# Two chained blocks on one core: silu of block two's convolution channels on ScalarE, a third value buffer, and later slots on TensorE for the sums of squares

## The reference, cut to what matters

```
u = rms_norm(h, norm_mix)
proj = u @ w_in                                   # 1024 x (512 + 4*512 + 8)
pool_out = pool_mixer(proj[..., :P], w_pool, pool_scale)
qkv = causal_conv_silu(proj[..., P:P + 3*G], conv_w)      # 4 taps over time, then silu
z = proj[..., P + 3*G:P + 4*G];  a, b = the last 8 columns
q, k are then l2-normalised per head of 128 channels: t * rsqrt(sum(t*t) + EPS)
```

## Time and profile before

| | |
|---|---|
| three runs, us | 2588.22, 2595.64, 2595.78; median 2595.64 |
| profiled execution | 2589.21 us, of it 2587.5 us span |
| busy shares | PE 93%, PEld 74%, DVE 71%, ACT 42%, POOL 28% |
| mean granted TensorE clock | 0.971 of full speed |
| first tap of channel 5 to first tap of channel 13 | 1452.22 to 1571.34 us of the span |

### The profile page before, as it was taken

The page is one execution under the profiler, slowest core; times in us unless marked ns, Lnnn a source line. Parts: engine busy times, 40 slices in busy tenths (PEclk is TensorE's granted clock), DMA queues, the critical chain, the costliest instruction groups (busy, mean ns, idle before and its releaser), DMA issues.

```text
span 2587.5 us, 35017 instructions
## 1 busy us (share of the span) xinstructions
PE 2396.1 (93%) x13848; PEld 1905.2 (74%) x13848; DVE 1829.8 (71%) x2431; ACT 1075.7 (42%) x1616; POOL 721.2 (28%) x737
## 2 busy tenths in 40 slices
PE   3988969879999999999999999888999999999998
PEld 3966823457778788888887767677787878888887
DVE  6358988885577798778865685466447678877775
ACT  5135468854343344433343442233234334444333
POOL 1432277505455211111032223323453310000000
PEclk8999979989999999999999999999999999999999
DMA  6200155224223545454433111001231353555542
GB/s 234 74 17 17 42 147 127 83 66 141 70 67 122 189 137 191 175 187 150 133 99 112 36 38 33 2 2 35 66 122 57 114 203 131 187 179 179 174 145 80
DMA packets 173850, 282.20 MB, mean 109 GB/s; under 512 B 13407, under 2 KB 86900, under 8 KB 173686
## 3 DMA queue, kind: packets, MB, share of 16 engines
q1 hardware_dynamic: 160336, 259.57, 30.9%
q10 hardware_dynamic: 13350, 20.38, 2.2%
HBM read 252.52 MB, written 27.33 MB: 108 GB/s over the span
## 4 chain that ended last, share of the span: by engine, by line
PE 72%; DVE 14%; issue 5%; ACT 5%; POOL 4%; DMA 1%; SPq 0%; ACTq 0%; DVEq 0%; POOLq 0%
PE ps L2927 20%; PE ps L2916 16%; PE ps L2621 5%; PE ps L2622 5%; PE ps L2623 5%; PE ps L2606 4%; PE ps L2608 3%; PE ps L2607 3%; PE ps L3096 2%; DVE yt L2429 2%; PE ps L2697 1%; DVE w_lo L2132 1%; DVE yt L2418 1%; DVE raw L2149 1%; PE ps L2777 1%
## 5 line engine op out<-in xcount | busy, mean ns | idle before, releaser
L1471 ACT ACTIVATE w_hi<-raw 128x1024 fp32r<-128x1024 f32 x198 | 209.0, 1057 | 366.9 <-DVE raw L2149 163.4
L2132 DVE TENSOR_TENSOR w_lo<-raw,w_hi 128x1024 fp32r<-128x1024 f32 x198 | 259.5, 1311 | 126.2 <-ACT w_hi L1471 125.9
L2927 PE MATMUL ps<-w_hi,us_hi 128*128 128x512 f32 x784 | 308.8, 394 | 15.4 <-DVE u_f L2158 9.9
L2927 PE MATMUL ps<-w_lo,us_hi 128*128 128x512 f32 x784 | 308.0, 393 | 0.0
L2927 PE MATMUL ps<-w_hi,us_lo 128*128 128x512 f32 x784 | 307.4, 392 | 0.0
L2606 PE MATMUL ps<-h_hi,w_hi 128*128 128x512 f32 x704 | 286.7, 407 | 8.8 <-issue 4.3
L2608 PE MATMUL ps<-h_hi,w_lo 128*128 128x512 f32 x704 | 276.4, 393 | 0.0
L2607 PE MATMUL ps<-h_lo,w_hi 128*128 128x512 f32 x704 | 276.3, 393 | 0.0
L2182 DVE TENSOR_TENSOR x<-x,ps 128x512 f32<-128x512 f32 x392 | 247.4, 677 | 0.1
L1033 POOL TENSOR_TENSOR raw<-raw,gate 128x1024 f32<-128x1024 f32 x32 | 93.6, 2946 | 378.0 <-DMA raw<-in_w_down_dram 378.0
L2927 PEld LDWEIGHTS ps<-w_hi,us_hi 128*128 128x128 f32 x784 | 147.7, 188 | 53.2 <-DVE u_f L2158 11.6
(11 more groups left out here) (488 smaller groups left out, 5318.3 us busy)
## 6 DMA issues: line engine op xcount, KB each, us to landing
h_all<-h_t SPq DMA_DIRECT2D x96, 512.0 KB, 5.5
h_extra<-h_t SPq DMA_DIRECT2D x96, 512.0 KB, 6.7
raw<-in_w_up_dram SPq DMA_DIRECT2D x64, 512.0 KB, 3.9
raw<-in_w_down_dram SPq DMA_DIRECT2D x64, 512.0 KB, 6.2
raw<-in_w_ada_dram SPq DMA_DIRECT2D x48, 512.0 KB, 4.2
raw<-in_w_in_dram SPq DMA_DIRECT2D x32, 512.0 KB, 3.8
raw<-in_w_out_dram SPq DMA_DIRECT2D x32, 512.0 KB, 3.9
h_t<-ht_hi ACTq DMA_DIRECT2D x32, 256.0 KB, 2.3
```

The costliest lines, as they stand in the source:

```text
L1471: s.activation(w_hi[:, slot, :], raw[:, r, :], ACT.Copy).then_inc(sem("w_hi_done"), 1)
L2132: v.tensor_tensor(w_lo[:, slot, :], raw[:, r, :], w_hi[:, slot, :].bitcast(F32), ALU.subtract).then_inc(sem("split_done"), 1)
L2927: last = mm(ps[:, b, :], l[:, c, tok], r, start=(fresh and c == 0 and n == 0), stop=(c == 1 and n == 2), skip_group_check=True)
```

## The change: what it does

ScalarE evaluates silu itself (`ACT.Silu`) where it evaluated the sigmoid, so VectorE's product at L2433 is dropped and `conv_silu` is counted by ScalarE. The value buffer of channel i becomes one of three; the third is `zc[:, 0, :]`, which is free until channel 16 but for the pool groups' intermediate values. The first tap of channel i waits for channel i - 3 instead of i - 2. On TensorE the product into banks 6 and 7 of channel j stands before `cm` of channel j + 2 for pool groups 0 to 2 (the same place in the stream as before), and inside `cm` of channel j + 2 for the others: after 4 of its 16 steps for pool group 3, after 2 of them for q and k.

```
-                y = yt[:, i % 2, :]
+                y = y_of[i]
...
+        AUX_STEP = {i: 0 for i in range(GH - 1)}
+        AUX_STEP[GH - 1] = 4
+        AUX_STEP.update({GH + j: 2 for j in range(2 * GH)})
+        y_of = [(yt[:, 0, :], yt[:, 1, :], zc[:, 0, :])[i % 3] for i in range(len(CH2))]
...  (ScalarE)
-                    if i >= 2 and ch_free[i - 2]:
-                        act.wait_ge(sem(ch_free[i - 2][0]), ch_free[i - 2][1])
+                    if i >= 3 and ch_free[i - 3]:
+                        act.wait_ge(sem(ch_free[i - 3][0]), ch_free[i - 3][1])
...
                     act.wait_ge(sem("taps"), 3 * (c + 1))
-                    s.activation(chunk_of(c), y, ACT.Sigmoid).then_inc(sem("conv_sig"), 1)
+                    s.activation(chunk_of(c), y, ACT.Silu).then_inc(sem("conv_silu"), 1)
...  (VectorE)
-                if i < len(CH2) and kind == "qkv":
-                    dve.wait_ge(sem("conv_sig"), c + 1)
-                    v.tensor_tensor(chunk_of(c), chunk_of(c), y, ALU.mult).then_inc(sem("conv_silu"), 1)
...  (TensorE)
+            def aux(i):
+
+                kind, c = CH2[i]
+                if i == 0:
+                    pe.wait_ge(sem("ab_out"), 2)
+                elif (i - 1) in aux_read:
+                    pe.wait_ge(sem(aux_read[i - 1][0]), aux_read[i - 1][1])
+                y = y_of[i]
+                if kind == "pool":
+                    pe.wait_ge(sem("gs_in"), 48)
+                    pe.wait_ge(sem("pooled"), 2 * (c + 1))
+                else:
+                    pe.wait_ge(sem("l2_sq"), c + 1)
+                for half in range(2):
+                    last = mm(ps[:, 6 + half, :], wpool[:, c, :] if kind == "pool" else ones,
+                              y[:, half * HALF:(half + 1) * HALF], start=True, stop=True)
+                last.then_inc(sem("pool_mm" if kind == "pool" else "l2_mm"), 1)
+
+            def aux_in(i, half):
+
+                def after(k):
+                    if AUX_STEP.get(i - 2) == NK * half + k + 1:
+                        aux(i - 2)
+                return after
+
+            for i in range(len(CH2)):
+                if AUX_STEP.get(i - 2) == 0:
+                    aux(i - 2)
...
-                        cm(i, half, 2 * (i % 3) + half, None, "cm2_full", 2 if i == 0 else None)
+                        cm(i, half, 2 * (i % 3) + half, aux_in(i, half), "cm2_full", 2 if i == 0 else None)
```

More of the change, by code:

```diff
@@ L1630, in aux_out, with first_tap @@
                                  bias=eps2 if c < GH else eps).then_inc(sem("l2_sd"), 1)
+            def first_tap(i):
+                c = CH2[i][1]
+                s.activation(y_of[i], pair(i), ACT.Copy,
+                             scale=cw2[:, 3 * 12 + c:3 * 12 + c + 1]).then_inc(sem("tap0"), 1)
             for i in range(len(CH2) + 1):
@@ L1643, in _ @@
                     if kind == "qkv":
-                        s.activation(y, pair(i), ACT.Copy,
-                                     scale=cw2[:, 3 * 12 + c:3 * 12 + c + 1]).then_inc(sem("tap0"), 1)
+                        first_tap(i)
                     if kind == "z":
@@ L2426, in _ @@
                     if kind1 == "qkv" and c1 < 2 * GH:
-                        y1 = yt[:, (i - 1) % 2, :]
+                        y1 = y_of[i - 1]
                         dve.wait_ge(sem("l2_sd"), c1 + 1)
@@ L3032, in _ @@
             pe.wait_ge(sem("norm_lo"), 5 * NK + 6)
-            for i in range(len(CH2) + 1):
+            def aux(i):
[4 more added lines that the diff above has]
+                    pe.wait_ge(sem(aux_read[i - 1][0]), aux_read[i - 1][1])
+                y = y_of[i]
+                if kind == "pool":
[15 more added lines that the diff above has]
+                    aux(i - 2)
                 if i < len(CH2):
@@ L3055, in _ @@
                     mm(ps[:, 6, 32:64], blk, g32, start=True, stop=True).then_inc(sem("gs_mm"), 1)
[L3056 to L3071, removed]
             pe.wait_ge(sem("z_silu"), GH - 1)
```

## The result

The changed kernel takes 2573.89 us in the median of six runs, the kernel before 2588.8 us in the median of six; the medians lie 14.9 us apart. The ratio, which is that of the means of these runs, is 0.9934, with a 95% interval of 0.9917 to 0.9951. That is 17 us less (13 to 21 by the interval). The profiled execution took 2572.14 us, with a span of 2570.4 us.

What follows compares the result with a forecast made beforehand. PE was taken to bound most of the kernel, a loop through ACT and DVE the eight q and k rounds; 8 x 12.65 = 101.2 instead of 119.12 us gains 17.9, so 2595.64 - 17.9 = 2577.7, forecast 2577, range 2569 to 2584.

Steps and rivals of the forecast that it cites:

- The hole and its loop: Eight q and k rounds: a loop through ACT and DVE makes periods of 14.89 us, PE waiting 11.4 us for squares.
- Sum: Eight q and k rounds at PE's pace, 101.2 instead of 119.12 us; the whole 17.9 us reach the end.
- Silu: ACT in each round: silu taken at 1.06 us like the sigmoid; only over 5.8 us would it lengthen the period.
- Table loads: ACT: if silu is in another set, beta's sigmoid and first z add one load each in idle time, cost 0.
- The order within a round: Times after T, the end of `cm` of a channel on PE; DVE has 1.0 us of slack each round.
- The later slot and the third buffer: Sums of squares inside channel i + 1 on PE, price 1.75 us as before; third buffer cost 0.
- Masks: GpSimd, behind v's last silu: masks take 13.4 us, and 11.6 us of slack before first use stays.
- Rival A: q and k rounds: hand-overs eat the slack, the loop becomes DVE's, 13.5 us gained, 2582; chance 0.08.
- Rivals B to E: B: product dearer inside channels, 2590, 0.06; C: lost later, 2581, 0.04; D: clock falls, 2679, 0.02; E: unchanged, 2595, 0.03.

Runs made afterwards that it cites:

- the one-pass sums: Changed kernel with q and k squares rounded to fp32r and summed by two one-pass matmuls instead of four float32 passes: 2561.93 us, ratio 0.9895; with old slot 2560.08.
- the same cut by order alone: Kernel before with only VectorE's silu product moved ahead of the reciprocal, two buffers, old slot: 2587.85 us, one run.

## Why the prediction was right

The forecast was 2577 us, 0.993 of the kernel before, and the measured ratio is 0.9934. By its own steps:

- *The hole and its loop.* Right. Rounds of 14.89 us became 12.65, and the run with DVE's load restored outside the loop lost nothing.
- *Sum.* 17.9 us were worked out, 17.94 lie between the first taps. Outside them the profiled execution is 1.42 us longer ahead and 0.6 us shorter behind, within the scatter of the executions. The absolute time lies 3 us lower than forecast. The median of before, 2595.64 then, is 2588.8 with three more runs, and 2588.8 - 17.9 would be 2570.9; the median of the changed kernel lies 3 us over that. How near 2577 came to it is thus in part a matter of the scatter. The sum against the profiled execution gave 2571.3, and 2572.14 was measured.
- *Silu.* 1.06 us, as the nearest row. The Trainium skill, "ScalarE: Activation LUTs", "Step-by-step: what each stage is for", says that the function doesn't change the throughput, and the trace agrees.
- *Table loads.* Silu and sigmoid are in different sets: beta's sigmoid got a load at 1450.04 and the first z one at 1582.77. Both lie in idle time, as forecast. The load again starts 0.02 us after the instruction before it, and the next, where it need not wait for another engine, 0.01 to 0.02 behind it; the drain that the Trainium skill adds in "ScalarE: Activation LUTs", "What ACT_TABLE_LOAD costs", is not seen.
- *The order within a round.* The product on PE was put at T+1.4, the square root at T+3.3 and the end of the square at T+7.9, with 1.0 us of slack on DVE. With T = 1466.04, a quarter before the first tap, the rows have T+1.4, T+3.3 and T+7.9, and 1.01 us.
- *The later slot and the third buffer* were each costed at 0 for the path. Right, but the slot's reason was not needed: at its old place the sum costs nothing either in the kernel with silu alone, and 0.37 us with the one-pass sums.
- *Masks.* They start at 1582.81 and end at 1596.16, used at 1609.02: 12.9 us of slack, 11.6 forecast; the silu of v comes a little earlier because the product on DVE is gone.

Where it was wrong is in the rivals. Rival A and the slack it rests on charged any round of DVE over 12.65 us at once to the end: "8 x 1.7 = 13.5 us gained". Silu alone ran 12.88 us rounds, and the run with one more product 12.8 to 15.1 on DVE, at no cost. The slack of 1.0 us is only that of the first tap; PE needs the square 5 to 6 us after it is ready, and a lag has to use that up before PE waits. I had the 6 us in the text ("6 us earlier") and did not use it in the rival. Rivals B to E are not seen: the product takes 1.88 us within a channel as between two, the stretch from z to the end is no longer, the clock rose to 1.00, and no wait of PE took the place of the old one.

## What to carry to other kernels

When two engines take turns in hand-ordered streams, look for the loop through both: here one short product behind a long reciprocal held the next round's first instruction, and 18 us came from cutting that, not from the work saved. Then look for the loop that is next in length: with two buffers the same cut by order alone gave 2.3 us. Count slack to the engine that sets the end, and over all rounds: a round that is 0.2 us too long for eight rounds costs nothing when 5 us are in hand. The other parts of an edit may then be idle, as the third buffer was, until the bound moves: with PE's round 1.3 us shorter it carried 7 us.

## What was not expected of the hardware

DVE and GpSimd held each other up, and which of them lost depended on who came first. A DVE product of two SBUF tiles (1.22 us alone) that started while a GpSimd cast or subtraction was under way took 1.44 to 3.44 us, longer the more of that was still to come, and ended 1.07 to 1.09 us behind it, in all such cases of the twelve profiles but one, where both records start at the same time. The row of DVE in the changed kernel with one-pass sums:

```profile
1490.80 3.31 DVE L2443 TENSOR_TENSOR qc<-qc,yt 128x1024 f32<-128x1024 f32 x1
```

and the GpSimd instruction that it met:

```profile
1490.63 2.40 POOL L1119 TENSOR_TENSOR w_lo<-raw,w_hi 128x1024 fp32r<-128x1024 f32 x1
```

In the kernel before it was GpSimd's cast, started 0.05 us behind DVE's product at 1464.92, that took 2.07 instead of 1.04 us:

```profile
1464.97 2.07 POOL L1110 CAST w_hi<-raw 128x1024 fp32r<-128x1024 f32 x1 [9.12 <-PE ps L2608]
```

So each seems to wait for the other's whole instruction. Which of them starts first can hang on a few hundredths of a microsecond, and the longer products account for the odd rounds above (13.56, 15.74, 17.44 and 18.30 us). The Trainium skill, "GPSIMD Engine Reference", "Specifications", lists SBUF interfaces shared with VectorE and contention with DVE instructions that have two SBUF inputs, and the traces agree. The taps, which read PSUM and SBUF, showed no such growth, 3.90 to 3.92 us for three in every kernel.
